# Long convolution by cosine and sine sums: folded transforms, with the filter tiles placed between projections

## The reference, cut to what matters

```python
uc = short_conv_centred(u_hy, hy_conv_w, hy_conv_b)
x0, x1, vh = jnp.split(uc, 3, axis=-1)
filt = (hdn @ w4).reshape(T, 2, 1024) * window      # hdn: three sine layers
h_f, h_b = filt[:, 0], filt[:, 1]
z = x1 * vh
g = concatenate([h_f, 0, h_b[:0:-1]])               # n = 2T
y = irfft(rfft(z, n) * rfft(g, n), n)[:T]
y_b = (x0 * (y + z * hy_skip)) @ w_hy_out
```

## Time and profile before

| | us |
|---|---|
| median of 3 runs | 1984.39 (1984.2 to 1988.61) |
| profiled execution | 1983.55 |
| its span | 1981.7 |
| TensorE busy | 1625.5 (82% of the span), mean granted clock 0.924 |
| VectorE busy | 1255.5 (63%) |
| ScalarE busy | 1000.6 (50%) |
| GpSimd busy | 263.9 (13%) |
| HBM | 243 GB/s over the span |

### The profile page before, as it was taken

One profiled execution on the slowest core, in us unless ns is written; L12 is line 12 of the kernel. 1 busy time (PEld: TensorE's weight loads), 2 busy tenths in 40 slices (PEclk: granted clock), 3 DMA queues, 4 the chain that ended last, 5 costly groups with the idle time before them and its releaser, 6 DMA issues.

```text
span 1981.7 us, 43798 instructions
## 1 busy us (share of the span) xinstructions
PE 1625.5 (82%) x19979; PEld 1225.1 (62%) x19979; DVE 1255.5 (63%) x733; ACT 1000.6 (50%) x622; POOL 263.9 (13%) x137
## 2 busy tenths in 40 slices
PE   4898999898999999984568787778876787777974
PEld 3553773487868888873566565655565565654652
DVE  4423343247235233334699888989889988899884
ACT  4231133132213222222487777777677777777763
POOL 0405041403000000000007301101011000101000
PEclk9799999899999999995789899989899999899987
DMA  9000210112200725122799999999999999999993
GB/s 324 22 22 0 77 58 0 64 44 85 86 0 22 291 94 170 54 79 94 311 361 408 402 410 406 408 412 412 402 403 415 409 409 404 404 416 408 422 406 122
DMA packets 107994, 482.43 MB, mean 243 GB/s; under 512 B 5867, under 2 KB 51243, under 8 KB 91212
## 3 DMA queue, kind: packets, MB, share of 16 engines
q1 hardware_dynamic: 102656, 467.94, 60.0%
q0 software_dynamic: 4704, 12.98, 2.4%
q10 hardware_dynamic: 556, 0.32, 0.1%
HBM read 470.48 MB, written 10.75 MB: 243 GB/s over the span
## 4 chain that ended last, share of the span: by engine, by line
PE 37%; DMA 32%; DVE 14%; ACT 9%; issue 6%; POOL 2%; SPq 0%; ACTq 0%; DVEq 0%; POOLq 0%
PE ps_all L1047 23%; DMA slot<-in_w_exp_gate 15%; DMA slot<-in_w_exp_down 15%; DVE wl L985 8%; ACT wh L644 6%; PE ps_all L1070 5%; PE ps_all L1128 4%; DVE tmp L826 1%; PE ps_all L1114 1%; POOL qk L427 1%; PE ps_all L1232 1%; ACT wh L638 1%; POOL tmp L419 1%; POOL psp L424 1%; DMA xg<-xn_rows,tok 1%
## 5 line engine op out<-in xcount | busy, mean ns | idle before, releaser
L985 DVE SCALAR_TENSOR_TENSOR wl<-slot,wh 128x4096 f16<-128x4096 f32 x184 | 809.2, 4422 | 98.9 <-ACT wh L644 98.6
L644 ACT ACTIVATE wh<-slot 128x4096 f16<-128x4096 f32 x184 | 664.3, 3616 | 223.4 <-DMA slot<-in_w_exp_down 104.1
L1269 PE MATMUL ps_all<-xcur,wl 128*128 128x66 f16 x4096 | 421.7, 198 | 183.7 <-ACT sg L650 103.5
L1269 PEld LDWEIGHTS ps_all<-xcur,wl 128*128 128x128 f16 x4096 | 397.5, 102 | 200.1 <-ACT sg L650 105.1
L1270 PE MATMUL ps_all<-xcur,wh 128*128 128x66 f16 x4096 | 421.4, 199 | 6.5 <-issue 6.5
L1271 PE MATMUL ps_all<-xcur,wh 128*128 128x66 f16 x4096 | 420.7, 200 | 6.5 <-issue 6.5
L1270 PEld LDWEIGHTS ps_all<-xcur,wh 128*128 128x128 f16 x4096 | 397.5, 100 | 6.8 <-issue 6.5
L1271 PEld LDWEIGHTS ps_all<-xcur,wh 128*128 128x128 f16 x4096 | 397.6, 101 | 3.1 <-issue 3.1
L1047 PE MATMUL ps_all<-xnt,wsp 128*128 128x272 f16 (+1 forms) x2688 | 309.8, 278 | 7.0 <-DVE rot L860 5.2
L1047 PEld LDWEIGHTS ps_all<-xnt,wsp 128*128 128x128 f16 x2688 | 264.9, 99 | 52.4 <-issue 8.4
L1283 PE MATMUL ps_all<-wh,hidt 128*66 128x512 f16 x480 | 182.6, 380 | 23.7 <-DVE wl L985 23.4
...
...
...
## 6 DMA issues: line engine op xcount, KB each, us to landing
...
slot<-in_w_exp_up SPq DMA_DIRECT2D x64, 2048.0 KB, 21.4
...
```

Source lines behind the costliest of these rows:

```text
L644: nc.scalar.activation(wh[c % RING][:, :], slot[(c + 2) % SLOTS][:, :], ACT.Copy, scale=W_S).then_inc(S["w_hi"], 1)
L985: nc.vector.scalar_tensor_tensor(wl[c % RING][:, :], slot[(c + 2) % SLOTS][:, :], W_S, wh[c % RING][:, :], ALU.mult, ALU.subtract).then_in ...
L1269: nc.tensor.matmul(dst, lo, xcur[:, k, 0, :], start=k == 0 and t % TIL == 0, stop=False, skip_group_check=True)
```

## The change

- The transforms use symmetry. GpSimd makes z(264 + n) + z(263 - n) and their difference (zeo), 264 times each, reading the second half backwards. The cosine part of Z needs the sum only, the sine part the difference only: three time tiles of 88 rows each. 24 transposes, 90 matmuls.
- The filter's times are put in the order even, odd: six tiles of 88 rows, three even, three odd. For a frequency f and its mirror T - 1 - f the even and odd partial sums enter with one sign and with the other. So four jobs `G` (two frequency tiles x cosine or sine) hold the even sum in one bank and the odd one in the other, 18 matmuls each; ScalarE copies the odd one, VectorE writes both frequency tiles. A job `GM` does the 16 middle frequencies in full, 36 matmuls.
- Frequency tiles now are 128, 128, 16, 128, 128 (FS).
- Sum and difference of the two filters go into w4 at the start (two VectorE operations), so that the matmuls give them at once; GpSimd's sums L403 and L404 go. The filter tiles stand behind the first three projections of part 1, two behind each.
- Products: two sets of four buffers; VectorE does the sum, GpSimd the difference and both low parts.
- `Y`: cosine part in one bank, sine part in the other, 264 columns each, 30 matmuls per output. All four outputs do frequency tiles 0 to 3 first, then all four do tile 4. VectorE adds the banks to both halves of the output, with four operations per output, two of them backwards.
- Tables: dft_g, two dft_z and dft_y in place of dft_f and dft_i; the window has six tiles.

The diff, cut, and moved eight columns to the left:

```diff
...
+HT = T // 2
+KT = HT // 3
+NK = T // KT
+FS = [(0, 128), (128, 128), (256, 16), (272, 128), (400, 128)]
+GF = 272
...
+FL_AT = ((0, 1), (2, 3), (4, 5), ())
...
-    if part == 0:
-        for k in range(NT):
-            add(("FL", hf, k), "filt_win", hf * NT + k + 1)
+        if part == 1:
+            for k in FL_AT[i]:
+                add(("FL", hf, k), "filt_win", 2 * (hf * NK + k) + 2)
     if part == 1:
-        for f in range(NT):
-            add(("G", hf, f), "g_evac", hf * NT + f + 1)
-        for k in range(NT):
-            add(("ZT", hf, k), "zt_split", hf * NT + k + 1)
+        for g in range(4):
+            add(("G", hf, g), "g_fold", hf * 4 + g + 1)
+        add(("GM", hf), "g_mid", hf + 1)
+        for k in range(3):
+            add(("ZT", hf, k), "zt_split", hf * 3 + k + 1)
         for f in range(NT):
             add(("Z", hf, f), "z_mul", hf * NT + f + 1)
...
+tmz = tmp + [sb(f"tmz{i}", [128, HALF], F32, TOP + 29248 + 2048 * i) for i in range(4)]
...
-            sp.dma_start(dft_f[:, :, :, :], A["c_dft_f"]).then_inc(S["dft_fwd"], 16)
-            sp.dma_start(dft_i[:, :, :, :], A["c_dft_i"]).then_inc(S["dft_inv"], 16)
+            sp.dma_start(dft_g[:, :, :, :], A["c_dft_g"]).then_inc(S["dft_fwd"], 16)
+            for a in range(2):
+                sp.dma_start(dft_z[a][:, :, :, :], A["c_dft_z"][a]).then_inc(S["dft_fwd"], 16)
+            sp.dma_start(dft_y[:, :, :, :], A["c_dft_y"]).then_inc(S["dft_inv"], 16)
...
+        for k in range(NK):
             for i, dst in enumerate((fp_, fm_)):
+                n = 2 * (hf * NK + k) + i
+                pool.wait_ge(S["filt_hi"], n + 1)
+                nc.gpsimd.tensor_tensor(dst[0:KT, k, 1, :], tmp[2 * (k % 2) + i][0:KT, :], dst[0:KT, k, 0, :],
+                                        ALU.subtract).then_inc(S["filt_lo"], 1)
         pool.wait_ge(S["consts"], 48)
         for i in range(4):
             c = C_SK + 4 * hf + i
+            pool.wait_ge(S["u_used"], 12 * hf + 4 + i + 1)
+            if hf:
+                pool.wait_ge(S["tile_done"], AT[("ZT", 0, 2)] + 1)
+            nc.gpsimd.tensor_tensor(zeo[:, 0, i, :], zt_c[:, i, HT:T], zt_c[:, i, HT - 1::-1], ALU.add).then_inc(S["z_fold"], 1)
+            nc.gpsimd.tensor_tensor(zeo[:, 1, i, :], zt_c[:, i, HT:T], zt_c[:, i, HT - 1::-1], ALU.subtract).then_inc(S["z_fold"], 1)
+            pool.wait_ge(S["z_fold"], 8 * hf + 2 * i + 2)
             nc.gpsimd.tensor_scalar(zt_c[:, i, :], zt_c[:, i, :], par[:, c:c + 1], None, ALU.mult).then_inc(S["z_skip"], 1)
         for f in range(NT):
-            p = TS[f][1]
+            p = FS[f][1]
             n = hf * NT + f
+            tz = tmz[4 * (f % 2):4 * (f % 2) + 4]
             pool.wait_ge(S["z_mul"], n + 1)
+            nc.gpsimd.tensor_tensor(tz[0][0:p, :], tz[0][0:p, :], tz[1][0:p, :], ALU.subtract).then_inc(S["p_sub"], 1)
+            pool.wait_ge(S["p_hi"], 2 * n + 1)
+            nc.gpsimd.tensor_tensor(psp[0:p, f, 3, :], tz[2][0:p, :], psp[0:p, f, 2, :], ALU.subtract).then_inc(S["p_lo"], 1)
...
+                    if part == 1:
+                        for k in FL_AT[i]:
+                            for a, dst in enumerate((fp_, fm_)):
+                                act.wait_ge(S["filt_win"], 2 * (hf * NK + k) + a + 1)
+                                nc.scalar.activation(dst[0:KT, k, 0, :], tmp[2 * (k % 2) + a][0:KT, :], ACT.Copy).then_inc(S["filt_hi"], 1)
...
+                for g in range(4):
+                    act.wait_ge(S["tile_done"], AT[("G", hf, g)] + 1)
+                    if g >= 2:
+                        act.wait_ge(S["g_fold"], hf * 4 + g - 1)
+                    nc.scalar.activation(tmp[g % 2][:, :], pair(AT[("G", hf, g)], 512, 1024), ACT.Copy, scale=G_S).then_inc(S["g_odd"], 1)
+                j = AT[("GM", hf)]
+                p = FS[2][1]
+                act.wait_ge(S["tile_done"], j + 1)
+                nc.scalar.activation(gsp[0:p, 2, :, :].rearrange("p a n -> p (a n)"), pair(j, p=p), ACT.Copy, scale=G_S).then_inc(S["g_mid"], 1)
+                for k in range(3):
+                    j = AT[("ZT", hf, k)]
+                    act.wait_ge(S["tile_done"], j + 1)
+                    nc.scalar.activation(zt_t[0:KT, k, 0, :, :].rearrange("p a n -> p (a n)"), pair(j, p=KT), ACT.Copy,
...
+    def window(hf, k):
+        n, j = hf * NK + k, AT[("FL", hf, k)]
+        dve.wait_ge(S["tile_done"], j + 1)
+        if k >= 2 or hf:
+            dve.wait_ge(S["filt_lo"], 2 * n - 2)
+        if hf and k < 2:
+            dve.wait_ge(S["p_lo"], 2 * NT)
+        for i in range(2):
+            t = tmp[2 * (k % 2) + i]
+            ins = nc.vector.tensor_tensor(t[0:KT, :], pair(j, 512 * i, 512 * i + 512, KT), win[0:KT, k, :], ALU.mult)
+            if k == 0:
+                link(ins)
+                if i:
+                    nc.vector.tensor_tensor(tmp[0][0:1, :], tmp[0][0:1, :], t[0:1, :], ALU.add).then_inc(S["filt_win"], 2)
+            else:
+                ins.then_inc(S["filt_win"], 1)
...
+                        if i == 0:
+                            dve.wait_ge(S["win"], 16 * (hf + 1))
+                        for k in FL_AT[i]:
+                            window(hf, k)
...
+                    if c == 0:
+                        link(nc.vector.tensor_tensor(w4[:, 0:D], w4[:, 0:D], w4[:, D:2 * D], ALU.add))
+                        nc.vector.scalar_tensor_tensor(w4[:, D:2 * D], w4[:, D:2 * D], -2.0, w4[:, 0:D], ALU.mult, ALU.add).then_inc(S["w4_ready"], 1)
...
+            if part == 1:
+                for g in range(4):
+                    j, (part_, a) = AT[("G", hf, g)], divmod(g, 2)
+                    dve.wait_ge(S["g_odd"], hf * 4 + g + 1)
+                    odd = tmp[g % 2][:, :]
+                    link(nc.vector.scalar_tensor_tensor(gsp[:, part_, a, :], pair(j, 0, 512), G_S, odd, ALU.mult, ALU.add))
+                    if a == 0:
+                        ins = nc.vector.scalar_tensor_tensor(gsp[:, 3 + part_, a, :], pair(j, 0, 512), G_S, odd, ALU.mult, ALU.subtract)
+                    else:
+                        ins = nc.vector.scalar_tensor_tensor(gsp[:, 3 + part_, a, :], pair(j, 0, 512), -G_S, odd, ALU.mult, ALU.add)
+                    ins.then_inc(S["g_fold"], 1)
+                for k in range(3):
+                    n, j = hf * 3 + k, AT[("ZT", hf, k)]
+                    dve.wait_ge(S["zt_hi"], n + 1)
+                    nc.vector.scalar_tensor_tensor(zt_t[0:KT, k, 1, :, :].rearrange("p a n -> p (a n)"), pair(j, p=KT), Z_S,
+                                                   zt_t[0:KT, k, 0, :, :].rearrange("p a n -> p (a n)"),
+                                                   ALU.mult, ALU.subtract).then_inc(S["zt_split"], 1)
+                dve.wait_ge(S["filt_lo"], 2 * NK * (hf + 1))
+                dve.wait_ge(S["g_mid"], hf + 1)
+                dve.wait_ge(S["g_fold"], 4 * (hf + 1))
+                for f in range(NT):
+                    p, n, j = FS[f][1], hf * NT + f, AT[("Z", hf, f)]
+                    tz = tmz[4 * (f % 2):4 * (f % 2) + 4]
                     dve.wait_ge(S["tile_done"], j + 1)
+                    if f >= 2:
+                        dve.wait_ge(S["p_lo"], 2 * n - 2)
                     for t, (a, b) in enumerate(((0, 0), (1, 1), (0, 1), (1, 0))):
+                        ins = nc.vector.tensor_tensor(tz[t][0:p, :], pair(j, 512 * a, 512 * a + 512, p), gsp[0:p, f, b, :], ALU.mult)
+                    ins.then_inc(S["z_mul"], 1)
+                    dve.wait_ge(S["z_mul"], n + 1)
+                    nc.vector.tensor_tensor(tz[2][0:p, :], tz[2][0:p, :], tz[3][0:p, :], ALU.add).then_inc(S["p_sum"], 1)
                 dve.wait_ge(S["z_skip"], 4 * hf + 4)
+                y_s = 1.0 / (T * Z_S * F_S * G_S)
                 for i in range(4):
                     j = AT[("Y", hf, i)]
                     dve.wait_ge(S["tile_done"], j + 1)
+                    late, early = zt_c[:, i, HT:T], zt_c[:, i, HT - 1::-1]
+                    nc.vector.scalar_tensor_tensor(late, pair(j, 0, HT), y_s, late, ALU.mult, ALU.add)
+                    link(nc.vector.scalar_tensor_tensor(early, pair(j, 0, HT), y_s, early, ALU.mult, ALU.add))
+                    nc.vector.scalar_tensor_tensor(late, pair(j, 512, 512 + HT), y_s, late, ALU.mult, ALU.add)
+                    nc.vector.scalar_tensor_tensor(early, pair(j, 512, 512 + HT), -y_s, early, ALU.mult, ALU.add).then_inc(S["y_done"], 1)
...
+                if part != 1:
+                    continue
+                if hf == 0 and i == 0:
+                    pe.wait_ge(S["sin_ready"], 3)
+                    pe.wait_ge(S["w4_ready"], 1)
+                for k in FL_AT[i]:
                     n = begin(("FL", hf, k))
                     for a in range(2):
+                        last = nc.tensor.matmul(pair(n, 512 * a, 512 * a + 512, KT), hdn[:, KT * k:KT * k + KT],
                                                 w4[:, D * a + HALF * hf:D * a + HALF * hf + HALF], start=True, stop=True)
```

(53 more changed lines are left out.)

190 lines of the change are left out of this document (47 added, 143 removed).

## The result

Four executions of the changed kernel took 1899.05, 1901.17, 1923.01 and 1968.03 us; before, four took 1984.20 to 1988.61. The ratio is 0.9609, 95% interval 0.9538 to 0.968 (the comparison leaves the 1968.03 out): faster. I had said 1886, range 1874 to 1904, so the median of 1912.09 is outside. Six more executions in the first experiment gave 1898 to 1972, so the spread belongs to the kernel. The profiled execution took 1899.05 us, its span 1897.1.

What follows compares the result with a forecast made beforehand. Waits lay 37% on TensorE, 32% on DMA; TensorE bounds the stretch before the experts. Halves save 57.5 and 43.6 us, minus 3.4 for the clock: 97.7 off 1983.55 gives 1885.9, 1886.7 on the median's scale; predicted 1886, range 1874 to 1904.

Steps and rivals of the forecast that it cites:

- the clock charge: At Z's start, after the wait: the clock falls and costs 1.7 us in each half, 3.4 together.
- half clock through G and Z: Rival, chance 0.02: G, Z and the filter tiles run at clock 0.50 throughout; 1990 us, slower by 6.
- All waits cost more: Rival, chance 0.13: the four waits before Z and inside Y cost the clock 4.8 us each; 1902 us.
- The transposes' rival: Rival, chance 0.08: transposes and following wait count as idle, Z starts at half clock, each half loses 4.8 us; 1893.
- Filter tiles: Six 88-row tiles behind part 1's first projections: 10.7 us per half, full clock, 0.8 us wait for the sine.
- Before G: TensorE's wait for the last filter parts before G: 2.2 us in half 0, 0.5 in half 1.
- G and Z: Filter and z transform matmuls at 0.216 us each: G 23.3 us, Z 19.4 us per half.
- Transposes and wait: Between G and Z: 24 transposes, then copies and splits; Z starts 6.5 us after G.
- Y: Output transform: 14.4 us of matmuls and a 3.3 us wait for product tile 3, GpSimd's round being 4.5 us.
- Y's evacuation: Four VectorE operations per output, about 0.43 us each, hidden beside final matmuls and the next projection; nothing charged.
- rival on reversed operands: Reversed operands slow: double cost in Y's evacuation, 3.5 us more, still hidden; or GpSimd five times, 1908 us, chance 0.02.
- Behind the convolution: Everything behind 412.03 us starts on the same chain's semaphores, so the saving should reach the end whole.

Runs made afterwards that it cites:

- the first experiment: The changed kernel run again with nothing edited (also called the repeat): six executions from 1898.09 to 1971.51 us, the profiled one 1971.24.
- the filled kernels: Changed kernel plus dummy 128-row matmuls in TensorE's waits: before Z only, 1907.58 us; before G and Z, 1883.65, or 1884.04 with G and Z zero-padded to 128 rows.
- the kernel with only Z's wait filled: Changed kernel plus 15 dummy matmuls of 128 rows in the wait before Z, in both halves: 1907.58 us median.
- Z alone padded: Changed kernel with Z's matmuls at 128 rows instead of 88, the added rows zero, G's left at 88: median 1929.77 us.

## Why the prediction was wrong, point by point

**The step that failed: the clock charge**, "I charge 1.7 in both halves". The 1.7 came from Z's start before the change, where the stream behind the wait held 128-row tiles. Where the clock falls at the new Z's start it stays down to Z's end: 18.5 us in the profiled execution, and in the profiled repeat (1971.24) both G's and both Z's. I priced the fall and took the return for granted. With the return restored a fall before Z costs 1.7 and 1.6 us, as I charged (up to 3.0 in other profiles), and the time is 1886.5; without falls it is 1883.7 (ratios 0.9493 and 0.9485, too near for the times to tell apart).

That 1886.5 meets my 1886 is partly luck: in its profile the waits before G are 2.7 and 1.7 us longer than foreseen and G's fall costs 1.7 that I hadn't charged, which two shorter waits in Y (2.6 each) and before Z (0.8 each) take back.

**The rival that held it**, half clock through G and Z, got 0.02. Its own sum without the filter tiles, 1886.7 - 3.4 + 85.4 = 1968.7, is the upper group (1966 to 1971.5). I dismissed it because 16-row and 64-row matmuls had run at 1.00. That shows that few rows keep a clock, not that they regain one. The first row of that group spoke to the second: 64-row matmuls, 17.5 us without a gap, at 0.50 to the end. I had read it as what a long wait leaves behind.

**All waits cost more** (0.13, 1902): the waits that it priced at 4.8 each cost something else. The one in Y was 0.65 us and cost the clock nothing, the one before Z cost 18.5 or nothing. That 1902 is near some executions is chance.

**The transposes' rival** (0.08): the filled kernels keep 1.00 through 2.8 us of transposes and Z behind them, and where the clock stood at 0.50 before the transposes, it came back inside them: 2.9 us into them in the kernel with only Z's wait filled, 3.6 and 3.3 in the repeat, 3.4 and 4.2 with Z alone padded. The rule of the Trainium skill (TensorE: Matmul & The Clock Gate, Part 4: PE-mode transpose) is that they don't count as activity. These five stretches speak against it for this kernel's f32 transposes, since the 88-row matmuls ahead of them had left the clock at 0.50 for 45 us or more.

**Filter tiles:** two take 3.66 us at full clock (3.6 foreseen). "TensorE has no reason to be at half clock" was wrong in the profiled execution, 4.66 and then 7.88 for a projection. The wait for the sine was 0.71 us (0.8 foreseen), and the clock fell some 2.5 us behind it, inside the two tiles. It cost next to nothing at the end, as G waits for GpSimd.

**Before G:** 2.2 and 0.5 foreseen; 4.65 at full clock (1.63 in the slowed execution) and 1.98. The chain behind the third projection's chunk held 1.8 us more of GpSimd's low parts and 0.8 more of the split than I counted; together about the difference.

**G and Z:** 23.5 and 19.64 at full clock (23.3 and 19.4). 0.216 a matmul was right for 88 rows. **Transposes and wait:** 5.7 (6.5); VectorE's 1024-column split takes 1.21, less than twice 0.67.

**Y:** a wait of 0.65 where I had 3.3, and 14.40 busy, exact. VectorE and GpSimd do exclude each other; the first product tiles of half 0, in order of time:

```profile
139.43 0.69 DVE L866 TENSOR_TENSOR tmp<-tmp,tmp 128x512 f32<-128x512 f32 x1
139.48 1.77 POOL L431 TENSOR_TENSOR tmp<-tmp,tmp 128x512 f32<-128x512 f32 x1 [22.30 <-DVE tmp L863]
...
143.45 1.71 POOL L431 TENSOR_TENSOR tmz<-tmz,tmz 128x512 f32<-128x512 f32 x1
...
147.36 1.71 POOL L431 TENSOR_TENSOR tmp<-tmp,tmp 16x512 f32<-16x512 f32 x1
```

GpSimd's difference takes 1.77 beside VectorE's sum, 1.26 alone; the rule of the Trainium skill that I cited (SBUF — State Buffer, Who interferes with whom) agrees. But its round is 147.36 - 143.45 = 3.9 us, not 4.5: the exclusion cost 0.5 rather than 0.71, and there was no hand-over to add, since each operation starts as the last ends. Over four rounds that covers the 2.2 us by which tile 3 came earlier (155.30 - 132.72 = 22.6 us after Z's start, 24.8 foreseen).

**Y's evacuation** was free, and reversed operands no dearer than straight ones (busy us and mean ns of four, straight and then reversed):

```profile
L873 DVE SCALAR_TENSOR_TENSOR zt_c<-ps_all,zt_c 128x264 f32<-128x264 f32 x4 | 1.7, 425 | 9.9 <-PE ps_all L1211 9.9
...
L874 DVE SCALAR_TENSOR_TENSOR zt_c<-ps_all,zt_c 128x264 f32<-128x264 f32 x4 | 1.7, 421 | 0.0
```

GpSimd's reversed passes took 0.74 us each alone, so neither rival on reversed operands came in.

**Behind the convolution** the saving passed whole.
